# A hybrid decoder step: the sample dots are dealt out anew over the groups of the key phase, and the routing stands ahead of them

## The reference

```python
def block(xb):                                   # 128 tokens
    q = (xb @ w_q).reshape(128, 8, 2, 128)
    s = einsum('bhpd,hpkd->bhpk', q, sub_keys)
    sv, si = top_k(s, 16)
    cand = (sv[:, :, 0, :, None] + sv[:, :, 1, None, :]).reshape(128, 8, 256)
    cv, ci = top_k(cand, 16)
    i1 = take_along_axis(si[:, :, 0], ci // 16);  i2 = take_along_axis(si[:, :, 1], ci % 16)
    idx = i1 * 128 + i2;  gate = softmax(cv)
    act = gelu(einsum('bhkd,bd->bhk', u_emb[idx], xb))
    return einsum('bhk,bhkd->bd', gate * act, v_emb[idx])
```

## Time and profile before

| | |
|---|---|
| median of 3 runs | 2006.75 us (2006.36 to 2007.18) |
| the profiled execution's own time | 2009.67 us |
| its span | 2007.9 us |
| PE busy | 1896.3 us (94%) |
| DVE busy | 1482.6 us (74%) |
| ACT busy | 745.4 us (37%) |
| POOL busy | 741.0 us (37%) |

### The profile page before, as it was taken

The page is one execution under the profiler, slowest core; times in us unless marked ns, Lnnn a source line. Parts: engine busy times, 40 slices in busy tenths (PEclk is TensorE's granted clock), DMA queues, the critical chain, the costliest instruction groups (busy, mean ns, idle before and its releaser), DMA issues.

```text
span 2007.9 us, 35481 instructions
## 1 busy us (share of the span) xinstructions
PE 1896.3 (94%) x14267; PEld 1768.4 (88%) x14267; DVE 1482.6 (74%) x2765; ACT 745.4 (37%) x954; POOL 741.0 (37%) x600
## 2 busy tenths in 40 slices
PE   9998987888999999999999999988999999999997
PEld 8998976767459999999899998877999999999997
DVE  6616665775247779889899998876788777887777
ACT  6434544443032133445455454434232233223322
POOL 8235727560013201333433233442554334433440
PEclk9999978999999999999999999989999999999999
DMA  6212210020141235788999778989999999999993
GB/s 204 64 45 68 69 45 3 8 76 25 54 165 43 85 127 210 253 324 290 340 355 340 285 282 338 364 332 372 390 400 347 357 359 358 343 353 362 353 330 115
DMA packets 183781, 463.47 MB, mean 231 GB/s; under 512 B 15168, under 2 KB 92736, under 8 KB 173408
## 3 DMA queue, kind: packets, MB, share of 16 engines
q1 hardware_dynamic: 126480, 239.32, 34.1%
q0 software_dynamic: 46080, 167.79, 22.2%
q10 hardware_dynamic: 11088, 54.53, 6.7%
HBM read 398.45 MB, written 63.11 MB: 230 GB/s over the span
## 4 chain that ended last, share of the span: by engine, by line
PE 73%; DVE 13%; DMA 5%; ACT 4%; POOL 2%; issue 2%; ACTq 0%; SPq 0%; DVEq 0%; POOLq 0%
PE bank L2042 29%; PE bank L1957 15%; PE bank L1374 6%; PE bank L1911 5%; PE bank L1863 3%; DMA sca<-in_pu_rows,pick 2%; DMA sca<-in_pu_rows,gate 2%; DVE u_lo L2616 2%; DVE sca L2623 2%; PE bank L1394 1%; PE bank L1966 1%; PE bank L1933 1%; DVE hot_a L2710 1%; POOL sca L860 1%; ACT u_hi L1219 1%
## 5 line engine op out<-in xcount | busy, mean ns | idle before, releaser
L1957 PE MATMUL bank<-xhi,u_hi 128*128 128x416 f32 x1008 | 367.9, 365 | 7.5 <-DVE u_lo L2616 7.5
L2042 PE MATMUL bank<-w_hi,v_hi 128*128 128x416 f32 x1024 | 360.3, 352 | 4.6 <-DVE w_lo L2891 4.6
L2042 PE MATMUL bank<-w_hi,v_lo 128*128 128x416 f32 x1024 | 362.5, 354 | 0.0
L2042 PE MATMUL bank<-w_lo,v_hi 128*128 128x416 f32 x1024 | 358.5, 350 | 0.0
L1957 PE MATMUL bank<-xlo,u_hi 128*128 128x416 f32 x1008 | 356.7, 354 | 0.0
L1957 PE MATMUL bank<-xhi,u_lo 128*128 128x416 f32 x1008 | 356.2, 353 | 0.0
L860 POOL DMA_INDIRECT sca<-in_pu_rows,pick x128 | 174.7, 1365 | 421.1 <-DVE sdot L2623 310.4
L1302 ACT ACTIVATE v_hi<-v_raw 128x4096 fp32r<-128x4096 f32 x32 | 116.2, 3632 | 393.7 <-PE bank L2042 350.9
L2897 DVE TENSOR_TENSOR v_lo<-v_raw,v_hi 128x4096 fp32r<-128x4096 f32 x32 | 141.6, 4425 | 99.5 <-ACT v_hi L1302 99.5
L1957 PEld LDWEIGHTS bank<-xhi,u_hi 128*128 128x128 f32 x1008 | 192.4, 191 | 9.3 <-DVE u_lo L2616 6.8
L2042 PEld LDWEIGHTS bank<-w_hi,v_hi 128*128 128x128 f32 x1024 | 193.1, 189 | 6.1 <-issue 5.0
(11 more groups left out here) (692 smaller groups left out, 3758.2 us busy)
## 6 DMA issues: line engine op xcount, KB each, us to landing
u_raw<-in_pu SPq DMA_DIRECT2D x64, 1024.0 KB, 5.6
v_raw<-in_pv SPq DMA_DIRECT2D x128, 512.0 KB, 9.1
act_scratch<-actb ACTq DMA_DIRECT2D x64, 416.0 KB, 6.4
gate_scratch<-gst ACTq DMA_DIRECT2D x13, 2048.0 KB, 11.4
wts<-act_scratch SPq DMA_DIRECT2D x32, 832.0 KB, 6.7
gring<-gate_scratch SPq DMA_DIRECT2D x32, 832.0 KB, 13.3
wring<-in_w_q SPq DMA_DIRECT2D x4, 2048.0 KB, 8.9
wp_raw<-in_w_in SPq DMA_DIRECT2D x7, 1024.0 KB, 5.6
```

Of the source, the lines that this page charges most:

```text
L1957: ins = mm(bank[b][:, 0:VD], lhsT, rhs[:, 0:VD], **on)
L2042: ins = mm(bank[c][:, 0:VD], lhsT, rhs[q][:, e, 0:VD], **on)
```

## The change

Three tables and two pieces of code change. `HEAD_DOTS` goes from 6 to 8. The 142 other dots of blocks 0 to 48 (144 before) are dealt out by another list. In `one_hots` the routing of a block is put ahead of its dots. The routing of the last tile, which was in blocks 28 to 32, now goes over blocks 28 to 34. The sum of all dots stays at 160.

```diff
-HEAD_DOTS, TAIL_DOTS = 6, [5, 5]
+HEAD_DOTS, TAIL_DOTS = 8, [5, 5]
 XV = 32
-DOTS = [4 if j > 11 else 2 + j % 2 for j in range(16)] + [1 if j > 11 else 3 if j % 3 else 2 for j in range(16)] + [2, 3, 4, 4]
-DOTS += [3 if q == 4 else 4 for q in QUADS[36:]]
+BESIDE = [1, 4, 1, 4, 1, 4, 2, 4, 3, 1, 2, 4]
+DOTS = BESIDE + [4, 4, 4, 4] + BESIDE + [1, 1, 1, 1] + [2, 0, 2, 4] + [4] * 13
...
                     if j == 12:
                         candidates(last)
-                        best_pairs(last, 0)
-                    if j == 13:
-                        best_pairs(last, 2)
-                        best_pairs(last, 4)
-                    if j == 14:
-                        best_pairs(last, 6)
+                    best_pairs(last, 2 * (j - 12))
+                    if j == 15:
                         shift_gates(4, last)
-                        positions(last)
-                    if j == 15:
-                        find_places(last)
-                        place_keys(last)
                     return
                 if pos == 3:
                     if j == 0:
+                        positions(ORDER[4])
+                    if j == 1:
+                        find_places(ORDER[4])
+                        place_keys(ORDER[4])
+                    if j == 2:
                         sum_keys(ORDER[4])
                         norm_gates(4, ORDER[4])
                     return
...
                     if quad + 1 == QUAD0[j + 1]:
+                        if pos < 4:
+                            between(pos, j - (G0[pos] - HEAD0))
                         for r in range(DOT0[j], DOT0[j + 1]):
                             sample_dot(r)
-                        if pos < 4:
-                            between(pos, j - (G0[pos] - HEAD0))
                         j += 1
```

## The result

| | before | after |
|---|---|---|
| median | 2006.55 us (4 runs) | 2023.7 us (4 runs) |
| lowest and highest | 2003.95 to 2007.18 | 2018.95 to 2029.08 |
| profiled execution's own time | 2009.67 | 2029.08 |
| its span | 2007.9 | 2027.4 |

The ratio is 1.0079 [1.006, 1.0099], 12 to 20 us slower. The changed kernel ran again beside other runs: 2024.32 against 2007.9, ratio 1.0069 [1.0046, 1.0092].

What follows compares the result with a forecast made beforehand. It took TensorE's key-phase waits for late DVE, overloaded beside routing or awaiting gathered rows, as what counts. Terms -6.6 + 6.8 + 2.5 + 7.1 = +9.8 us on 2006.75 gave 2016.5, range 2004 to 2024.

Steps and rivals of the forecast that it cites:

- the last rival: A new wait after blocks 7 and 23: 2028 us, or 2022 at one place; chance 0.14 (slower still).
- Part 1: Fewer dots beside the routing remove nearly all six TensorE waits there: 6.6 of 7.1 us off.
- part 5: Stores after blocks 3, 7, 15, 19, 23, 27 and 31: no wait, costed at 0.
- Part 2: Eight dots in the head: group 12's `u_lo` waits for late rows, 5.0 us of wait plus 1.8 of clock, 6.8.
- Row 7: The gathered row for the head's dot 7, expected to land 11.8 us after issue, at 831.2.
- the lower bound's reason: Head: group 14's 1 MB load now issues later, out of the gathers' way, worth up to 2.5 us: wait 3.8.
- rival A: Rows land in time, so only the routing gain of -6.6 us is left: 2000.2 us; chance 0.13.
- Part 3: Block 11 has four dots, putting three of block 12's rows in a store's wake: +2.5 us on group 25's wait.
- Part 4: Four dots in blocks 38, 42 and 48: +3.7 on group 52, +2.0 after block 42, +1.4 before group 63; together 7.1.
- The stores after blocks 35 and 45: no change: Those stores have four dots on both sides before and after the change, so no added wait.
- Clock: Part of a group after a long wait runs at 1.2 GHz, priced at 1.8 us per new long wait.
- The value phase: Expected to keep its length, 601 us from 1406.95 to the end of the span.

Runs made afterwards that it cites:

- run 6: The changed kernel without 12 of its 13 gate stores, for timing only: 1990.85 us, ratio 0.9926 to the kernel before.
- after_again: The changed kernel run once more, unaltered, beside other runs, its trace used as a second sample: 2024.32 us, ratio 1.0069 to the kernel before.
- runs 1 and 2: Changed kernel with 6 head dots again: 2018.31 us, ratio 1.0054; kernel before with 8 head dots, none in block 0: 2010.74 us, ratio 1.0023.
- Run 3: Changed kernel with 3 dots instead of 4 in blocks 38, 42 and 48, the three moved to blocks 29, 33 and 34: 2022.66 us, ratio 1.0077.
- head6: Changed kernel with 6 dots in the head again, dots 6 and 7 going into blocks 0 and 2: 2018.31 us, ratio 1.0054.

## Why the prediction was right in its direction and short in its size

It said 2016.5 us, in a range from 2004 to 2024, and slower with a chance of 0.66. Measured were 2023.7 and 2024.3: slower, +17 us where +9.8 was forecast. The first median lies 0.3 us inside the range and the second 0.3 outside, and that the upper end was so high is owed to the last rival at one place (2022), which is about what happened.

- **Part 1, fewer dots beside the routing: right.** -6.5 and -7.4 us for -6.6. Without stores all waits for `hot_a` but one of 0.4 us are gone (run 6). It said under 1 us of waits from 925 to 950 and from 1000 to 1200 us; there were 1.4 us in the first stretch, those of group 21 and the group behind it, and in the second 3.6 in group 37 (part 5) and 0.8 in group 28.
- **Part 2, the head: right in mechanism and size.** The wait is 4.48 us, in after_again 5.27 (5.0 was taken), and the clock's part 3.0 and 2.8 (1.8 was taken), shown from both sides by runs 1 and 2. Row 7 came 10.1 us after its issue instead of 11.8; that fits the lower bound's reason, a load that no longer stands in the way, but no run separates it. In the changed kernel the two rows were issued at 814.86 and 817.07 and landed at 825.3 and 827.1, 10.5 and 10.1 us later, and rival A fell with that. By the Trainium skill ("DMA: Bandwidth & Descriptors", "Anatomy of one DMA — SWDGE (gpsimd) path"), about 2.0 us plus the bytes at 436 GB/s, they would have been there by 818.1 and 820.3, an estimate; the trace does not agree.
- **Part 3, group 25: right**, +3.1 and +2.9 for +2.5; the last of the four rows landed 17.5 us after the store (17.6 in after_again), 17 was said.
- **Part 4, a fourth dot in the last tile: right in sum**, 6.6 us in both for 7.1. Group 52 was taken too high (its last row landed 15.3 us after the store, not 17.1) and group 56 too low, so part of the agreement is luck. Run 3 shows the terms group by group; the kernel's time didn't show them, because the dots were dear where they went instead.
- **Part 5 is the step that failed.** "No wait" after blocks 7 and 23 was right for 7 and wrong for 23: +5.1 and +4.6 in group 37. The mechanism had been named as a rival, with 4 us of wait and 1.8 of clock a place (measured 3.6 and 1.5, in after_again 2.9 and 1.7). The premise was that a gather issued 2 us before a store is not in its wake. That came from one row, 2.08 us before. In the traces of all runs gathers issued 1.3 to 2.7 us before a store go both ways, 4 to 7 us or 8 to 11 and more; before itself has one at 1.39 us that took 6.2 and one at 1.27 that took 11.3. Such a place should have had a price between, not 0.
- **"The stores after blocks 35 and 45: no change" failed for 35.** The dots had not changed, but blocks 33 and 34 had routing put into them, and the gathers of block 35 began 1.7 us later against their store, so that three of them and not two were in the wake. I counted the dots and not when they start. +2.9 and +1.6 in group 49.
- **Group 21, +1.2**, is in these two profiles the slow issue on ACT's queue (2.08 and 1.95 us), which no part had.
- **Clock.** My sum had a price for it in the head only. PE's busy time grew by 4.5 us in the key phase, of which the head has 3.0, group 37 1.5 and group 56 1.2, with 1.0 less in group 63. Group 49 ran at the lower level in part already before (12.2 us busy, 12.5 now).
- **The value phase** kept its length within 0.7 us in after_again (606.3) and was 3.8 us longer in the profile above.

What stays open: why head6 has two levels of time 9 us apart, and how much of a saving in the key phase the value phase keeps. What decides whether a gather issued 1.3 to 2.7 us before a store falls into its wake stays open as well. The times of nearly every kernel scatter by 9 to 22 us (before itself went from 1998.32 to 2016.12 in one call), which fits waits that come and go in the same place from one execution to the next, but no run separates that.

## What to carry to other kernels

Before moving work between stages, list the large stores and, for each, which gathers are issued within 3 us ahead of it or behind it, and when each must be there; a start 1 or 2 us later can be enough for one gather more in the wake, and up to 2.7 us ahead of a store this case does not tell which way a gather goes. Count instructions per block last: the kernel that gave each block as much as VectorE had room for lost 17 us, the one that gave three instead of four in most blocks around the stores (and had other ends) won 20. A price that hangs on such a place is worth its chance times its size, not zero. And a gain in one phase is only a gain if the first work of the next phase isn't pushed behind it, so read both lengths.

## What the runs showed of the hardware

- In the trace of after the first gather in the wake of a 2 MB store landed 8 to 13 us after the store (mostly 10), the second 11 to 16, the third 15 to 19 and the fourth 17 to 21. Over all traces, a gather issued up to 1.2 us before the store was always slow (9 us or more), and one issued 1.3 to 2.7 us before it was slow or not. Taking the stores out hardly moves the median of a gather's time, though, 7.0 to 6.8 us; it is the few in the wake that TensorE waits for. DMA issues from 850 to 1400 us, of before, then of before without stores (count, KB each, median us to landing):

```profile
gate_scratch<-gst ACTq DMA_DIRECT2D x13, 2048.0 KB, 11.4
...
sca<-in_pu_rows,pick POOLq DMA_INDIRECT x114, 7.0
```

```profile
sca<-in_pu_rows,pick POOLq DMA_INDIRECT x118, 6.8
```

- Issuing the second store right behind the first on one queue can hold the engine for 2.08 to 2.35 us instead of 0.44 (in the changed kernel at 916.29 and 958.38, and 1.08 at 1008.74; in the kernel before at most 1.41, at 1001.27), which delays the compute instruction behind it.
- A wait of 4.48 us was followed by a group that ran 2.9 us longer without any wait: the loss after a long wait can be two thirds of the wait. In after_again it was half: 5.27 us, then 2.6.
